# First attention with one buffer of scores and two of turned probabilities, and a weight split put off at the ends of two down projections

## What is computed

```python
def ffn_sublayer(x, mod, k, g_pre, g_post, w_gu, w_down):
    h = adaln_in(x, g_pre, mod[k], mod[k + 1])
    return adaln_out(x, swiglu(h, w_gu, w_down), g_post, mod[k + 2], HALF_STEP)

# the first attention: 16 heads, 4 kv heads, head size 64; keys are the 256 tokens under a band, and 256 of the context
s = concatenate([q @ k_window.T + band_mask, q @ k_context.T, sink])
p = softmax(s);  o = p[..., :nk] @ v_window + p[..., nk:nk + C] @ v_context
yx = o.reshape(B, S, Q_DIM) @ w_o

# second block
gate, up = split(rms_norm(x, g_ffn) @ w_ffn_in);  x = x + (silu(gate) * up) @ w_ffn_out
x = x + sigmoid(rms_norm(x, g_ple) @ w_ple_gate) * (p @ w_ple_proj)
```

## Time and profile before

| | us |
|---|---|
| median of three runs | 2305.96 (2303.64 to 2308.48) |
| the profiled execution | 2303.21 |
| its span | 2301.9 |
| TensorE busy | 2167.0 (94%) |
| VectorE busy | 1496.0 (65%) |
| ScalarE busy | 1041.5 (45%) |
| DMA, mean over the span | 165 GB/s |

### The profile page before, as it was taken

One profiled execution on the slowest core, in us unless ns is written; L12 is line 12 of the kernel. 1 busy time (PEld: TensorE's weight loads), 2 busy tenths in 40 slices (PEclk: granted clock), 3 DMA queues, 4 the chain that ended last, 5 costly groups with the idle time before them and its releaser, 6 DMA issues. The chain is left out here.

```text
span 2301.9 us, 35343 instructions
## 1 busy us (share of the span) xinstructions
PE 2167.0 (94%) x14614; PEld 1950.0 (85%) x14614; DVE 1496.0 (65%) x2423; ACT 1041.5 (45%) x1677; POOL 120.5 (5%) x83
## 2 busy tenths in 40 slices
PE   5999999899999999989999998876999899999998
PEld 3988889898889888889888898746999787799998
DVE  4765776677566667766667766573566566777665
ACT  4622224653574222366322335464544444655444
POOL 1000000100210000020000001001000101000000
PEclk9999999899999999999999998888999899999999
DMA  7545555445445455554445554301465452244544
GB/s 287 183 166 194 191 174 174 147 171 193 149 145 181 169 201 183 172 176 147 172 169 208 178 174 159 126 19 56 150 220 183 160 211 92 74 152 170 195 171 144
DMA packets 70881, 378.79 MB, mean 165 GB/s; under 512 B 7488, under 2 KB 12480, under 8 KB 44096
## 3 DMA queue, kind: packets, MB, share of 16 engines
q1 hardware_dynamic: 67824, 369.92, 45.9%
q10 hardware_dynamic: 2896, 6.60, 0.8%
HBM read 375.45 MB, written 1.05 MB: 164 GB/s over the span
## 5 line engine op out<-in xcount | busy, mean ns | idle before, releaser
L516 PE MATMUL ps_g<-h,w_hi 128*128 128x256 f32 (+1 forms) x4288 | 1003.1, 329 | 26.7 <-DVE h L991 23.2
L903 DVE TENSOR_TENSOR w_lo<-w_raw,w_hi 128x1024 fp32r<-128x1024 f32 (+2 forms) x614 | 690.7, 1127 | 410.6 <-ACT w_hi L1477 409.7
L1477 ACT ACTIVATE w_hi<-w_raw 128x1024 fp32r<-128x1024 f32 (+2 forms) x614 | 591.7, 968 | 600.6 <-PE ps_g L516 457.3
L516 PEld LDWEIGHTS ps_g<-h,w_hi 128*128 128x128 f32 x4288 | 727.9, 192 | 102.3 <-DVE h L991 17.0
L516 PE MATMUL ps_g<-h,w_lo 128*128 128x256 f32 (+1 forms) x2144 | 701.5, 327 | 0.0
L516 PE MATMUL ps_g<-hid,w_hi 128*128 128x256 f32 (+1 forms) x2368 | 493.1, 307 | 3.1 <-DVE y L1071 2.1
L516 PEld LDWEIGHTS ps_g<-h,w_lo 128*128 128x128 f32 x2144 | 412.0, 192 | 35.5
L516 PEld LDWEIGHTS ps_g<-hid,w_hi 128*128 128x128 f32 x2368 | 383.9, 190 | 26.5 <-DVE w_lo L903 2.6
L516 PE MATMUL ps_g<-hid,w_lo 128*128 128x256 f32 (+1 forms) x1184 | 361.9, 306 | 0.0
L516 PE MATMUL ps_g<-b_h,w_hi 128*128 128x256 f32 x1504 | 287.1, 291 | 5.7 <-DVE b_h L1006 5.3
L516 PEld LDWEIGHTS ps_g<-b_h,w_hi 128*128 128x128 f32 x1504 | 233.2, 191 | 18.6 <-issue 16.5
(11 more groups left out here) (254 smaller groups left out, 1622.0 us busy)
## 6 DMA issues: line engine op xcount, KB each, us to landing
w_raw<-in_gu SPq DMA_DIRECT2D x130, 1024.0 KB, 4.8
mod_raw<-in_w_mod SPq DMA_DIRECT2D x128, 512.0 KB, 3.5
w_raw<-in_conv_cu SPq DMA_DIRECT2D x16, 1024.0 KB, 4.7
w_raw<-in_dn00b SPq DMA_DIRECT2D x16, 768.0 KB, 4.3
w_raw<-in_dn01b SPq DMA_DIRECT2D x16, 768.0 KB, 4.2
w_raw<-in_dn10b SPq DMA_DIRECT2D x16, 768.0 KB, 4.2
w_raw<-in_conv_out SPq DMA_DIRECT2D x8, 1024.0 KB, 4.8
w_raw<-in_w_in_a SPq DMA_DIRECT2D x8, 1024.0 KB, 4.8
```

The costliest lines, as they stand in the source:

```text
L516: mm = pe.matmul(at, w[wp][:, k, m * P:(m + 1) * P], acts[ap][:, k, cs], start=(k == 0 and n == 0 and not (one_bank and m)), stop=(k == kc ...
L903: dve.tensor_tensor(w_lo[u % 2][:, cols], w_raw[u % 2][:, cols], w_hi[u % 2][:, cols].bitcast(F32), ALU.subtract).then_inc(lo_made, 1)
L1477: act.activation(w_hi[u % 2][:, cols], w_raw[u % 2][:, cols], ACT.Copy).then_inc(hi_made, 1)
```

## The change

The first attention gets one buffer of scores (`ps_g` banks 0 and 1) and two of turned probabilities (`ps_s` banks 2 and 3, `ps_g` banks 2 and 3). At the ends of down projections, where unit L + 2 is larger than unit L, `low_ahead(L - 1)` and `high_ahead(L - 1)` are left out of `turns` and done first thing in `low_put_off(L)` and `high_put_off(L)`.

```diff
+def grows(u):
+
+    return UNITS[u].elems > UNITS[u - 2].elems or UNITS[u - 2].phase == "ple_proj"
...
-    att1 = attention_plan(items1, hid1, 0, 0, [ps_g[:, 0:2, :], ps_g[:, 2:4, :]],
+    att1 = attention_plan(items1, hid1, 0, 0, [ps_g[:, 0:2, :]],
                           [gate_tmp[:], sq[:], q_flat[:, 0], q_flat[:, 1]],
-                          [ps_s[:, 2:4, :]], [prod[:], ssum[:]])
+                          [ps_s[:, 2:4, :], ps_g[:, 2:4, :]], [prod[:], ssum[:]])
...
         def low_put_off(u):
+            if grows(u + 2):
+                low_ahead(u - 1)
             low_half(u + 2, 1)
             low_ahead(u)
...
             for u in us:
-                turn_of(u, hid, last_off and u == us[-1])
-                if not (last_off and u == us[-1]):
+                late = last_off and u == us[-1]
+                turn_of(u, hid, late)
+                if not (late or last_off and u == us[-2] and grows(u + 3)):
                     low_ahead(u)
...
         def high_put_off(u):
+            if grows(u + 2):
+                high_ahead(u - 1)
             high_half(u + 2, 1)
             high_ahead(u)
```

More of the change, by code:

```diff
@@ L1477, in high_half @@
                 act.activation(w_hi[u % 2][:, cols], w_raw[u % 2][:, cols], ACT.Copy).then_inc(hi_made, 1)
-        def grows(u):
-            return UNITS[u].elems > UNITS[u - 2].elems or UNITS[u - 2].phase == "ple_proj"
         def high_split(u):
```

## The result

The changed kernel takes 2295.24 us in the median of seven runs, the kernel before 2305.16 in the seven beside it. That is 12 us, between 9.5 and 14.5. A second comparison later gave 0.9956 (0.9941 to 0.9971). The forecast, 8.75 us or 0.9962, a median of 2297.2, lies just outside the first interval and inside the second. The span of the profiled execution went from 2301.9 to 2290.4 us.

The account below looks back on a forecast made before the run. TensorE was busy 94% of the span, but a loop of waits, no engine full, bounded the first attention. Savings of 5.7 (attention) + 2.3 + 0.75 (fourth, fifth FFN) = 8.75 us took 2305.96 to 2297.2; range 2293.0 to 2302.0.

Parts of the forecast that it names:

- ten steady pairs: First attention, pairs 5 to 15: 37.17 us falls to 32.05, saving 5.1 us (between 2.2 and 6.2).
- start of the attention: First attention's start: scores wait for the single score buffer, losing 0.5 us (from 3.4 lost to 0.8 gained).
- end of the attention: Last maximum to output projection: pair 14's turn no longer waits for a copy, saving 1.1 us (0 to 1.3).
- fourth FFN's end: Last down projection result taken when its matmul ends, before the put-off split: 2.3 us saved (1.0 to 2.4).
- fifth FFN's end: Result taken 4 us earlier, mostly hidden by the ple projection; TensorE's wait before the sums goes: 0.75 us (0 to 0.8).
- steady loop: First attention, scores to scores two pairs later: the turn leaves the loop, 7.43 to 6.41 us, 3.21 a pair.
- slower rival: First attention: TensorE's clock swings to 1.2 GHz for half of eleven pairs, 16.2 us lost, 2313.4 in all; chance 0.05.

Follow-up runs that it names:

- banks only: Kernel before with only the first attention's buffer change (one of scores, two of turned probabilities): 0.9977 of before, 5.3 us faster (3.2 to 7.4).
- splits only: Kernel before with only the put-off splits at the ends of the fourth and fifth FFN: 0.9977 of before, 5.3 us faster (2.8 to 7.6).
- one-buffer kernel: Kernel before with one buffer of scores and one of turned probabilities in the first attention: 1.0008 of before, 1.8 us slower.
- copy-first kernel: Changed kernel with ScalarE's copy of turned probabilities ahead of the step's exponents in the first attention: 0.9953 of the kernel before.
- fifth FFN's split only: Kernel before with only the put-off split at the fifth FFN's end: 0.9986 of before, 3.2 us faster (1.2 to 5.3).

## Why the prediction was right, and where it was short

| term | forecast | trace of the changed kernel | by itself |
|---|---|---|---|
| ten steady pairs | 5.1 | 5.12 | 5.12 (banks only) |
| start of the attention | -0.5 | -0.4 | -0.3 (banks only) |
| end of the attention | 1.1 | 1.2 | 1.2 (banks only) |
| fourth FFN's end | 2.3 | 2.2 | 3.2 (splits only) |
| fifth FFN's end | 0.75 | 1.03 | 1.0 in its trace, 3.2 (1.2 to 5.3) timed |
| sum | 8.75 | 9.2 | |

**The attention.** The steady loop was right to the hundredth: 7.43 - 1.02 = 6.41, and 32.05 measured for five of them. The one-buffer kernel shows that it is the second buffer of turned probabilities that does it, and the copy-first kernel that 3.21 was the loop through ScalarE. At the start the sum from rows at 1.2 GHz held within 0.3 us: pair 4's maximum was forecast near 1518.6, 13.9 us behind the first, and came at 1518.53, 13.7 behind it. Pair 5's came 16.89 us behind the first, where it was 16.53. At the end the turn of pair 14 waits for its normalisation (0.61) and no more for a copy, as forecast.

That the start cost 0.4 us and not more is in part luck, for it rests on where the clock fell in the kernel before. The kernel with the put-off splits only has the same banks there. In both traces TensorE has a gap of 2.21 us before the turn of pair 1. Behind it the clock fell in the one and not in the other; PE's scores of pair 3 and the window, first in the kernel before, then with the splits only:

```profile
1515.70 2.08 PE L613 MATMUL ps_g<-y 64*128 64x512 f32 x4
1514.00:1519.00 5.00, 5.00 (x33) 2.83 (x33) 1.84 (x5) 1.93 (x6) 0.00 (x0) 0.66 0.00 0
```
```profile
1515.78 1.13 PE L618 MATMUL ps_g<-y 64*128 64x512 f32 x4
1514.00:1519.00 5.00, 5.00 (x54) 3.56 (x53) 3.08 (x13) 2.89 (x7) 0.00 (x0) 1.00 0.00 0
```

Pair 5's maximum is 14.96 us behind the first there (16.54 with the fifth FFN's split only, which has the same banks too). Against 16.83 to 17.03 us in the three traces with the new banks and the old order, one score buffer costs 0.3 to 2.1 us at the start, and over the stage (107.3 to 107.9 us against 112.1 to 113.5) the banks save 4.2 to 6.2 us.

**The fourth FFN.** The gap shrank by 2.29 us, and 0.1 of it was lost behind the norm. Here too the clock varies: the stage is 26.2 us in three traces without the edit and 27.7 in the fourth (one buffer of each), and 23.9 to 24.0 in three with it and 23.0 to 23.4 in the other three.

**The fifth FFN** is the term that was mis-sized. "Between 0 and 0.8" took the 0.75 us gap of one profile as the most that could go. From the end of the ple projection to that of the first gate unit it takes 7.03 us in all seven traces that have the edit, and 8.06, 8.43 and 9.83 in the three without it: 1.0, 1.4 and 2.8. The gap itself is 0.75, 1.08 and 1.02 there. With the gap, TensorE's step from its last matmul before to the sums is 0.91 us longer from start to start (1.03 and 0.12), the sums themselves take 0.1 longer, and in the third case the clock falls to 1.2 GHz just behind it, which is shown by the window of the one-buffer kernel, 0.84, against 1.00 in the kernel before (that of the one-buffer kernel first):

```profile
2275.00:2286.00 11.00, 9.98 (x72) 9.78 (x72) 4.41 (x9) 7.27 (x10) 1.44 (x1) 0.84 0.30 100
```
```profile
2270.00:2281.00 11.00, 10.25 (x87) 10.05 (x86) 5.89 (x9) 7.80 (x10) 1.45 (x1) 1.00 0.28 99
```

So by these traces the edit is worth 1 to 3 us from execution to execution. How often each comes I don't know, since only profiled executions show it. The 3.2 us timed (1.2 to 5.3) fit the upper end better, but that they come from this stage is not shown.

**The rest of the 11.5 us** of the two spans, 2.3, lies where the change alters no instruction. 1.0 is in the gaps ahead of the ple projection (0.89 and 0.70, then 0.30 and 0.27), which vary in kernels with and without the edit. 1.3 is behind the second attention, where the granted clock was 0.80 before and 0.90 after; the same stretch took 105.6 to 105.7 us in all seven traces of kernels without the second score buffer, and 106.9, 107.1 and 104.3 in the three of kernels with it, so that it is not shown to be the change's:

```profile
1926.00:1943.00 17.00, 14.43 (x93) 12.34 (x94) 10.77 (x41) 6.01 (x20) 2.60 (x2) 0.80 0.18 63
```
```profile
1916.00:1933.00 17.00, 14.43 (x96) 11.81 (x95) 12.28 (x40) 7.07 (x21) 3.50 (x2) 0.90 0.17 63
```

Whether the timed runs hold more than the 9.2 us stays open: 12 us (9.5 to 14.5) in the first comparison, whose interval lies just above it, 10 (6.7 to 13.6) in the second. Banks only and splits only sum to 10.6.

**The slower rival**, the clock swinging in the attention, did not come in the steady part: the gaps went, and the granted clock stayed at 1.00. The Trainium skill (TensorE: Matmul & The Clock Gate, "A second HAM failure mode: psum-queue depth-cycling") says, of bf16 matmuls, that small idles between groups of matmuls make the clock swing between its two levels. The steady part does not bear this out: before the change a gap of 0.99 us stood in every second pair at a granted clock of 1.00, and afterwards there was no gap that could test it. At the start the trace agrees with the rule: with gaps of 1.54 and 1.40 us between scores the clock stayed at 1.2 GHz through three pairs, and without these gaps it was back before the turn of pair 0.

## What to carry to other kernels

When several engines are each 70 to 85% busy, write out one turn of the loop from row to row across the engines; the row that can leave it tells the gain, and the next busiest engine tells the floor. PSUM banks are best given to the buffer whose release closes that loop: here a second one for scores was worth nothing in the steady part and one for turned probabilities 0.51 us a pair. Where a buffer is needed only a few steps later, lend it to the start; and put what the next chain waits for ahead of work that is only wanted later, above all of work that itself waits for a DMA.

## What was not expected of the hardware

- A short gap of TensorE can cost more than its length, when the clock falls behind it: gaps of 1.08 and 1.02 us before the ple sums cost 1.4 us in one execution and 2.8 in another. Whether it falls changes from execution to execution: behind the same gap of 2.21 us at the start of the attention it fell in two traces and not in a third, which made 1.6 us.
- The same program reaches the first attention at quite different times. The two traces of the changed kernel differ by 8 us there, which is most of what the change brings, and TensorE is busy 9.3 us longer in the second, at a granted clock of 0.97 for 0.98:

```profile
0.00:1498.00 1498.00, 1423.37 (x8568) 1262.81 (x8568) 985.33 (x1401) 635.53 (x942) 84.29 (x58) 0.98 0.50 176
```
```profile
0.00:1506.00 1506.00, 1432.66 (x8568) 1270.92 (x8568) 985.37 (x1400) 635.17 (x942) 84.55 (x58) 0.97 0.50 175
```

A difference of two spans says little about an edit of this size; the length of the stage between the same two instructions was the same within 0.6 us.
